# Four norms of a first model: sums and inverse of the deviation kept one token to a partition, and spread again by TensorE

## The reference, cut to what matters

```python
def rms_norm(x, g):
    xf = x.astype(jnp.float32)
    y = xf * lax.rsqrt(jnp.mean(xf * xf, axis=-1, keepdims=True) + EPS)
    return (y * g.astype(jnp.float32)).astype(x.dtype)
...
        u = modulate(rms_norm(h, g_norm1[l]), mod[:, :, 0], mod[:, :, 1])
        uc = modulate(rms_norm(hc, g_norm1[l]), modc[0], modc[1])
        pl = jnp.split(u @ w_in[l], IN_SPLITS, axis=-1)
...
        u2 = modulate(rms_norm(h, g_norm2[l]), mod[:, :, 3], mod[:, :, 4])
        h = h + mod[:, :, 5] * conv_ffn(u2, w_up[l], conv_w[l], conv_b[l], w_down[l])
        if ctx_out:
```

## Time and profile before

| | |
|---|---|
| median of 3 runs | 3943.73 us (3940.05 to 3945.64) |
| the profiled execution's own time | 3943.65 us |
| its span, first to last instruction | 3941.6 us |
| mean granted clock of TensorE | 0.992 of full |
| busy share | PE 96%, PEld 77%, DVE 57%, ACT 40%, POOL 8% |

### The profile page before, as it was taken

One profiled execution on the slowest core, in us unless ns is written; L12 is line 12 of the kernel. 1 busy time (PEld: TensorE's weight loads), 2 busy tenths in 40 slices (PEclk: granted clock), 3 DMA queues, 4 the chain that ended last, 5 costly groups with the idle time before them and its releaser, 6 DMA issues. The chain is left out here.

```text
span 3941.6 us, 53696 instructions
## 1 busy us (share of the span) xinstructions
PE 3798.9 (96%) x20466; PEld 3041.6 (77%) x20466; DVE 2258.9 (57%) x3952; ACT 1567.2 (40%) x2679; POOL 315.0 (8%) x282
## 2 busy tenths in 40 slices
PE   7999989999999999999999999999899999999998
PEld 5876568888888888875788788877578887667887
DVE  5356677874543543365733555376657626766752
ACT  3245672213431322255722344353544425354431
POOL 0100001111000001100000100114010010400001
PEclk9999999999999999999999999999999999989999
DMA  5210015571121121200022233222023222212332
GB/s 193 81 43 26 1 49 165 171 237 57 65 69 60 62 70 57 70 25 26 10 98 82 84 97 100 102 89 93 19 87 99 96 91 94 80 33 90 97 101 81
DMA packets 81208, 320.13 MB, mean 81 GB/s; under 512 B 9728, under 2 KB 9856, under 8 KB 80128
## 3 DMA queue, kind: packets, MB, share of 16 engines
q1 hardware_dynamic: 68064, 270.49, 20.7%
q0 software_dynamic: 12960, 47.19, 3.6%
HBM read 311.09 MB, written 2.10 MB: 79 GB/s over the span
## 5 line engine op out<-in xcount | busy, mean ns | idle before, releaser
L539 DVE TENSOR_TENSOR split_low<-weight_ring,split_high 128x1024 fp32r<-128x1024 f32 (+1 forms) x352 | 470.1, 1335 | 417.9 <-ACT split_high L531 417.5
L531 ACT ACTIVATE split_high<-weight_ring 128x1024 fp32r<-128x1024 f32 (+1 forms) x364 | 405.5, 1115 | 751.2 <-PE banks L1522 341.1
L1722 PE MATMUL banks<-normed_high,split_high 128*128 128x512 f32 x1040 | 405.9, 390 | 3.0 <-DVE normed_low L1665 2.2
L1722 PE MATMUL banks<-normed_high,split_low 128*128 128x512 f32 x1040 | 404.9, 389 | 0.0
L1722 PE MATMUL banks<-normed_low,split_high 128*128 128x512 f32 x1040 | 404.9, 389 | 0.0
L2020 PE MATMUL banks<-normed_high,split_high 128*128 128x512 f32 (+1 forms) x704 | 237.9, 338 | 2.8 <-DVE normed_low L1935 2.7
L2020 PE MATMUL banks<-normed_low,split_high 128*128 128x512 f32 (+1 forms) x704 | 237.2, 337 | 0.0
L2020 PE MATMUL banks<-normed_high,split_low 128*128 128x512 f32 (+1 forms) x704 | 236.7, 336 | 0.0
L1722 PEld LDWEIGHTS banks<-normed_high,split_high 128*128 128x128 f32 x1040 | 195.2, 188 | 47.4 <-DVE normed_low L1665 3.0
L1722 PEld LDWEIGHTS banks<-normed_high,split_low 128*128 128x128 f32 x1040 | 195.2, 188 | 40.6
L1722 PEld LDWEIGHTS banks<-normed_low,split_high 128*128 128x128 f32 x1040 | 195.3, 188 | 39.9
(11 more groups left out here) (388 smaller groups left out, 8599.3 us busy)
## 6 DMA issues: line engine op xcount, KB each, us to landing
weight_ring<-in_up SPq DMA_DIRECT2D x174, 512.0 KB, 3.4
weight_ring<-in_down SPq DMA_DIRECT2D x64, 704.0 KB, 4.0
modulation_ring<-in_ada POOLq DMA_DIRECT2D x80, 512.0 KB, 3.8
weight_ring<-in_merge SPq DMA_DIRECT2D x48, 768.0 KB, 4.2
weight_ring<-in_inputs SPq DMA_DIRECT2D x36, 512.0 KB, 3.4
weight_ring<-in_out SPq DMA_DIRECT2D x32, 512.0 KB, 3.4
weight_ring<-in_xbc SPq DMA_DIRECT2D x16, 512.0 KB, 3.4
weight_ring<-in_short SPq DMA_DIRECT2D x12, 512.0 KB, 3.4
```

Of the source, the lines that this page charges most:

```text
L531: act.activation(k.splits[0][:, (n0 + panel) % RING, 0:width], k.slot(n0 + panel)[:, 0:width], ACT.Copy).then_inc(k.high_ready.sem, 1)
L539: dve.tensor_tensor(k.splits[1][:, s, 0:width], k.ring[:, s, 0:width], k.splits[0][:, s, 0:width].bitcast(F32), ALU.subtract).then_inc(k.l ...
L1722: last = pe.matmul(sums(r, half), w, x, start=(c + j == 0), stop=(c == KT - 1 and j == 2))
```

## The change

Squares are now stationary, 128 tokens at a time, and one column of ones is moved: token t of a group of 128 gets its sum on partition t, in one column of PSUM (`sum_columns`, 6 matmuls per tile for 768 tokens, 4 for 512). The root and the reciprocal are taken of 6 (or 4) columns in a new buffer `deviations`. Then TensorE spreads each column to all partitions again: the column, broadcast to 128x128, is stationary, and the identity is moved, 128 columns (`spread_inverse`, a new semaphore `inverse_spread`). VectorE's scaling reads the inverse from PSUM instead of SBUF, and waits for the spread. In norm 1 each tile's sums are followed by one filler matmul. The 12, 15, 18 and 16 fillers ahead of the first products become 2+4, 3+5, 3+6 and 3+5, with the spread between. `stream_norm` (norm 4) no longer calls `norm`, which itself stays as it was. The diff, cut (the second copies of like edits and the counts of semaphores at block ends are left out):

```diff
+def norm_by_columns(k, group, ranges, split=None, modulation=None, ahead=0, block=None):
...
+    @block.scalar
+    def _(act):
+        root_of_columns(k, act, SQUARES_BANK, (b - a) // P)
+        split_ahead(k, act, ahead)
+        for q, (src, dst, gain, shift) in enumerate(group if split else ()):
...
+        if modulation:
+            modulated_gains(k, dve, *modulation)
+        invert_columns(k, dve, (b - a) // P)
+        dve.wait_ge(*k.inverse_spread(1))
+        if modulation:
+            dve.wait_ge(*k.gains_ready(1))
+        for q, (src, dst, gain, _) in enumerate(group):
+            dve.scalar_tensor_tensor(dst[:, a:b], src[:, a:b], gain(which), k.psum[:, SQUARES_BANK, 0:b - a],
+                                     ALU.mult, ALU.mult).then_inc(k.scaled_ready.sem, 1)
+            if ahead == 2 and q == 0:
+                dve.wait_ge(*k.low_ready(1))
+                split_low(k, dve, k.next_panel, 1, KT * P, k.high_ready(2))
+            if split and q:
+                low_part(q - 1)
+        if split:
...
+def sum_columns(k, pe, bank, squared, count, start, stop):
+    for t in range(count):
+        last = pe.matmul(k.psum[:, bank, t:t + 1], squared[:, t * P:(t + 1) * P], k.table("ones")[:, 0:1],
+                         start=start and t == 0, stop=stop and t == count - 1)
+    return last
+def root_of_columns(k, act, bank, count, epsilon=12, at=0):
+    act.activation(k.deviations[:, at:at + count], k.psum[:, bank, 0:count], ACT.Sqrt,
+                   bias=k.scalars[:, epsilon:epsilon + 1], scale=1.0 / D).then_inc(k.deviation_ready.sem, 1)
+def invert_columns(k, dve, count, roots=1):
+    dve.wait_ge(*k.deviation_ready(roots))
+    dve.reciprocal(k.deviations[:, 0:count], k.deviations[:, 0:count]).then_inc(k.inverse_ready.sem, 1)
+def spread_inverse(k, pe, ready, targets):
+    pe.wait_ge(*ready)
+    for bank, first, count in targets:
+        for t in range(count):
+            last = pe.matmul(k.psum[:, bank, t * P:(t + 1) * P],
+                             k.deviations[:, first + t:first + t + 1].to_broadcast([P, P]), k.table("ident"),
+                             start=True, stop=True)
+        last.then_inc(k.inverse_spread.sem, 1)
...
             for n in range(squared):
                 pe.wait_ge(*k.squares_ready(n + 1))
-                for s, (a, b) in enumerate(columns):
-                    last = pe.matmul(k.psum[:, s, 0:b - a], k.table("ones"), k.probs[:, n % 2, a:b], start=(n == 0),
-                                     stop=(n == KT - 1))
-                last.then_inc(k.squares_summed.sem, 1)
+                sum_columns(k, pe, 0, k.probs[:, n % 2, :], T // P, n == 0, n == KT - 1).then_inc(k.squares_summed.sem, 1)
+                keep_busy(k, pe, 1)
             if ada:
                 modulate()
-            keep_busy(k, pe, 12 if ada else 18)
+            keep_busy(k, pe, 2 if ada else 3)
+            spread_inverse(k, pe, k.inverse_ready(1), ((0, CTX // P, LAT // P), (1, 0, CTX // P)))
+            keep_busy(k, pe, 4 if ada else 6)
             for c in range(KT):
...
-            for s, (a, b) in enumerate(columns):
-                act.activation(k.probs[:, 2, a:b], k.psum[:, s, 0:b - a], ACT.Sqrt, bias=k.scalars[:, 12:13],
-                               scale=1.0 / D).then_inc(k.deviation_ready.sem, 1)
+            root_of_columns(k, act, 0, T // P)
...
                     dve.scalar_tensor_tensor(scaled(c)[:, a:b], k.stream[:, c, a:b], k.gains[:, 0, c, s:s + 1],
-                                             k.probs[:, 3, a:b], ALU.mult, ALU.mult).then_inc(k.scaled_ready.sem, 1)
+                                             k.psum[:, s, 0:b - a], ALU.mult, ALU.mult).then_inc(k.scaled_ready.sem, 1)
...
-                invert()
+                invert_columns(k, dve, T // P)
...
-            dve.wait_ge(*k.inverse_ready(2))
+                invert_columns(k, dve, T // P)
...
+            if by_columns:
+                sum_columns(k, pe, plain_bank, squared_tiles[:, 2, :], n // P, True, False)
+            for region, (a, b) in enumerate(() if by_columns else squared_columns):
                 pe.matmul(k.psum[:, plain_bank + region, 0:b - a], k.table("ones"), squared_tiles[:, 2, a:b], start=True,
                           stop=False)
...
-        keep_busy(k, pe, 16 if late is None else 6)
+        if late is None:
+            keep_busy(k, pe, 3)
+            spread_inverse(k, pe, k.inverse_ready(0), ((SQUARES_BANK, 0, n // P),))
+            keep_busy(k, pe, 5)
+        else:
+            keep_busy(k, pe, 6)
...
         modulated_gains(k, dve, l, 1)
+        invert_columns(k, dve, T // P)
+        dve.wait_ge(*k.gains_ready(1))
         for q, (c, s, a, b) in enumerate(units):
             if c == 0:
-                dve.wait_ge(*k.deviation_ready(s + 1))
-                if s:
-                    low_part(q - 1)
-                dve.reciprocal(k.probs[:, 3, a:b], k.probs[:, 2, a:b]).then_inc(k.inverse_ready.sem, 1)
-                dve.wait_ge(*k.inverse_ready(s + 1))
-                dve.wait_ge(*k.gains_ready(1))
+                dve.wait_ge(*k.inverse_spread(s + 1))
             dve.scalar_tensor_tensor(target[:, c, a:b], k.stream[:, c, a:b], k.gains[:, 1, c, s:s + 1],
-                                     k.probs[:, 3, a:b], ALU.mult, ALU.mult).then_inc(k.scaled_ready.sem, 1)
+                                     k.psum[:, SQUARES_BANK + s, 0:b - a], ALU.mult, ALU.mult).then_inc(
+                                         k.scaled_ready.sem, 1)
             if q == 0:
                 dve.wait_ge(*k.low_ready(1))
                 split_low(k, dve, k.next_panel, 1, KT * P, k.high_ready(2))
-            if c:
+            if q:
                 low_part(q - 1)
         low_part(len(units) - 1)
-    k.ends(deviation_ready=2, inverse_ready=2, scaled_ready=len(units), high_ready=len(units),
-           normed_ready=len(units), gains_ready=1)
+    k.ends(scaled_ready=len(units), high_ready=len(units), normed_ready=len(units), gains_ready=1)
...
-        keep_busy(k, pe, 15)
+        keep_busy(k, pe, 3)
+        spread_inverse(k, pe, k.inverse_ready(1), ((SQUARES_BANK, CTX // P, LAT // P), (SQUARES_BANK + 1, 0, CTX // P)))
+        keep_busy(k, pe, 5)
...
-            for s, (a, b) in enumerate(streams):
-                pe.matmul(k.psum[:, s, 0:b - a], k.table("ones"), k.probs[:, m, a:b], start=start, stop=not start)
+            sum_columns(k, pe, 0, k.probs[:, m, :], T // P, start, not start)
```

69 lines of the change are left out of this document (46 added, 23 removed).

## The result

The changed kernel takes 3955.47 us (median of 7 runs, 3953.26 to 3957.87), the kernel before 3943.50 (7 runs, 3939.81 to 3946.14): a ratio of 1.0034, with a 95% interval of 1.0024 to 1.0043. So by the medians the change costs 10 to 12 us. The forecast was 3959 with a range of 3944 to 3970.

The account below looks back on a forecast made before the run. TensorE was taken to bound the kernel between norms, VectorE to end last ahead of the norms' first products. Terms +17.5, -1.7, 0 and 0 gave +15.8 on 3943.65: 3959, range 3944 to 3970 (the forecast's own 3955 to 3963).

Parts of the forecast that it names:

- Norm 1: Norm 1: column sums leave the clock low, TensorE becomes last, first scaling at 67.9 instead of 50.44; +17.5.
- The row that the prediction took it from: Attention, 3479 to 3485: TensorE busy 5.84 of 6 us, 3.06 of weight loads, clock at 0.50; read as loads not lifting it.
- the blend with 0.33: Norm 1: a sum's pair at half clock priced 0.225, between ends 0.116 and a cold load's 0.33; doubling gives 0.232.
- Norm 2: Norm 2: latents 0.6 later because the clock falls, context 2.3 earlier; together -1.7.
- the latents' 1.25: Norm 2, latents: gain of 1.25 from earlier scaling, against 1.9 lost to a falling clock.
- The context's 2.3: Norm 2, context: the second reciprocal's 1.75, 0.20 ahead of it and an estimated 0.35 of waits saved, whatever the clock does.
- Norm 3: Norm 3: -2.5 from earlier scaling, cancelled by 2.5 taken for a clock fall; 0, bounds -2.5 and +1.5.
- Norm 4: Norm 4: -1.15 from earlier scaling, limited by GpSimd's low part, a clock fall weighed in; 0, bounds -1.15 and +1.5.
- the second rival: Clock stays low in norm 1 but holds in norms 2 to 4: +10.3, 3954; chance 0.14.
- The rival that the clock rises within norm 1's sums: Norm 1: clock rises at 28.0, +4.0 there; 3940.5 if held later, 3946 if lost; chance 0.16.
- the one with pairs under 0.07: Norm 1: clock rises in the sums and a pair costs 0.06, half the price taken; 3934, chance 0.03.
- the one with 0.33 a pair: Norm 1: a pair takes a cold load's 0.33, 4.9 a tile, +27.5: 3970; the slower-still cases have chance 0.09.

Follow-up runs that it names:

- e2: The changed kernel without the one filler behind each of norm 1's tiles; 3945.21 us, ratio 1.0007.
- e3: The changed kernel with seven fillers ahead of norm 1's first sums, still one filler a tile; 3950.75 us, ratio 1.0022.
- e6: As e4, but twelve fillers ahead of norm 1's sums instead of seven; 3944.95 us, ratio 1.0007.
- e8: As e5, but norm 1's wide root is turned into columns, inverted narrow and spread, with fillers only behind the spread; 3938.07 us, ratio 0.9984.
- e7: The changed kernel run again without an edit, as its second set; 3952.83 us, ratio 1.0025.
- e5: As e1, plus fillers between the two tiles' sums: three each for norms 2 and 4, two for norm 3; 3939.17 us, ratio 0.9988.
- e9: As e8, with seven fillers ahead of norm 3's sums instead of four and three between the tiles instead of two; 3934.31 us, ratio 0.9981.
- e10: As e5, with norm 3 also as in the kernel before; 3936.77 us, ratio 0.9987.
- e4: The changed kernel with seven fillers ahead of norm 1's sums and three behind each tile instead of one; 3946.89 us, ratio 1.0017.
- e1: The changed kernel with norm 1 alone as in the kernel before; 3939.03 us, ratio 0.9993.

## Why the prediction was right, and where its terms were off

**Norm 1 (forecast +17.5, measured +15.2 at the first product).** The mechanism is shown from three sides: the clock did not rise in 20 us of pairs alone (e2), it fell under pairs with one filler (e3), and at full clock the same pairs took half as long (e6). The row that the prediction took it from the earlier trace rows was weaker evidence than it said: in that stretch at 0.50 TensorE also moved wide matmuls, four of 512 columns in 2.08 us from 3481.1, and at 3485.4 the clock rose among matmuls of the same kinds. The forecast was right, but it rested on less than e2 has since given it. The sizes: the sum's pair took 0.213 at half clock instead of 0.225, a tile 3.41 instead of 3.61, eight of them 1.6 less, of which a later start and a longer first and last tile took back 0.5; that is the error in L748's start (+14.8 for +16.0). L748 lost 1.3 instead of 2.0 (11.75 long against 10.48 in e6), because the rise came 2.6 us behind its start and not 4 (no row gave the 4; the start of the kernel before took 5.0, and e2's rise came 3.6 behind the start of L748). From the turned rows' last matmul to the first scaling it took 2.50 for 2.73. The sum's pair is 0.105 at full clock (e6) and twice that, 0.213, at half. So doubling holds, and what was off is the full-clock price of 0.116, taken from a pair with 64 columns moved; the blend with 0.33 only happened to bring 0.232 nearer to the truth. What bound norm 1 before was misread too: ahead of the scaling at 50.44 stood GpSimd's low part, which ends at 49.99, and not the reciprocals, which end at 48.62 (e8). It cost the forecast nothing, since after the change TensorE is last by far.

**Norm 2 (-1.7, measured -2.5).** The two parts were sized apart and both hold roughly. The clock fell, from 978.0 to 981.4, and the latents' 1.25 went almost exactly: -0.08 in the changed kernel, -0.34 in e7, and -1.03 in e5, where it held. I had it 0.6 slower: the fall missed the sums, which took 1.39 and 1.50. The context's 2.3 was 2.40, and is the steadiest number here: the eleven profiles with norm 2 changed lie between -2.36 and -2.41. All of it falls where the prediction had it: from the latents' first product until TensorE is through with the first panels of the context and moves 512 columns again it takes 18.50 (985.14 to 1003.64) instead of 20.89 (970.75 to 991.64). At the takeover the 1.75 reciprocal is gone, and VectorE goes from the last latent tile to the first of the context without idle:

```profile
992.26 0.75 DVE L2025 SCALAR_TENSOR_TENSOR normed_low<-normed,modulations,normed_high 128x512 fp32r<-128x512 f32 x1
992.92 0.48 DVE L2034 SCALAR_TENSOR_TENSOR normed<-residual_stream,norm_gains,banks 128x256 f32<-128x256 f32 x1
993.32 0.75 DVE L2025 SCALAR_TENSOR_TENSOR normed_low<-normed,modulations,normed_high 128x512 fp32r<-128x512 f32 x1
```

**Norm 3 (0, measured +0.3).** Right for its reason in this execution: -2.5 without the clock, and the fall from 1541.2 to 1548.0 took it all:

```profile
1540.25 4.45 PE L556 MATMUL banks<-ones_and_identity,probs 128*128 128x1 f32 x24 [1.09 <-POOL probs L2192]
1545.00 2.90 PE L587 MATMUL banks<-ones_and_identity 128*128 128x256 f32 x6 [0.30 <-PEq L2309]
1547.69 1.66 PE L578 MATMUL banks<-ones_and_identity,deviations 128*128 128x128 f32 x12
```

The sums were to take 2.8 and the three fillers 1.36. e9 puts it the other way round: with the clock held and 1.36 of fillers paid, norm 3 gives 1.5. But the 0 is one outcome of two: in e2 and e3, whose norm 3 is the changed kernel's, the fall lasted 3.4 us instead of 6.8, and norm 3 gave 1.2 and 1.3. That the loss taken, 2.5 of at most 4.3, met the gain so exactly is luck.

**Norm 4 (0, bounds -1.15 and +1.5; measured -1.08 and +0.02).** Both happened, in two executions of one kernel. VectorE again waits for GpSimd's low part (0.46 idle at 2232.81), as written, and the gain is the 1.15 forecast when the clock holds. In e5, e8, e9 and e10, with fillers between the sums, it was -1.07 or -1.08 in all four. That the fillers did it is shown by e8 alone: the other three had the fall at some 1720 behind which norm 4 kept the clock in the changed kernel and e3 without any filler.

**The sum (15.8, measured 11.7 between the spans).** Norm 1 was sized 2.3 too dear, norm 2 0.8, norm 4 1.1 in this execution, norm 3 0.3 too cheap, and the stretches between give the last 0.2. So 3955.5 for 3959 comes of four errors of which three point the same way; norm 4's is chance. The second set's 3952.83 lies below the forecast's own 3955 to 3963, though in its whole range. The result near 3954 is not the second rival come true, in which the clock holds in norms 2 to 4: by the time alone the two could not be told apart, but the trace shows the falls in norms 2 and 3. The rival that the clock rises within norm 1's sums is refuted by e2 and e3; the one with pairs under 0.07 by e6's 0.105; the one with 0.33 a pair by 0.213.

**The rule that activity releases the clock**, which the prediction takes from the Trainium skill, "TensorE: Matmul & The Clock Gate", section "What's actually happening", agrees with the first rises, 2.6 and 3.6 us into L748 (changed kernel, e2). What the prediction found open in it, e2 answers for its own case: 20.5 us of back-to-back weight loads with one-column matmuls went by at half clock.

**Open.** Norm 1's first product to norm 2 and what follows norm 4 differ by up to 5 us, once 8.5, from the kernel before, in code that no edit touched. Behind norm 4 the record of the clock bears out that falls account for most of it: over the twelve profiles the stretch grows by some 0.45 us for each us spent at 0.50, from 1710.5 with 47 us (e8) to 1719.3 with 67 us (e2). Between norms 1 and 2 the seven profiles with 6.8 us at 0.50 took 904.5 to 908.1, the five with 3.4 us 902.3 to 905.3, so there the clock explains a part. Whether this is why medians differ by 1 to 2 us more than the segments say is not shown, since only one execution of each kernel was profiled. Of e4 only one of the three long executions was profiled, so that the nine others kept the clock is inferred from their times.

## What to carry to other kernels

Swapping the operands of a sum, so that the data is the stationary side and one column moves, saves no time on TensorE where the data is wide: 12 pairs took 1.26 at full clock and 2.56 at half, where wide sums of the same tile took 1.29, and the clock stayed down or fell while they ran in the changed kernel, e2 and e3. It paid where few tiles are summed and a wide reciprocal on the critical engine goes away: 2.40 in norm 2 whatever the clock did, and in norm 3 from a loss of 0.3 to a gain of 1.5, by how long the clock was down (a loss of 1.2 where fillers came on top of the fall, e5 and e8). Before pricing such a change, ask of each stretch which clock it will run at, and price fillers as part of it. A filler that does not change the clock is a plain cost: one a tile cost 7 us here. And before taking reciprocals for what binds, look at what the other engines end at the same moment: norm 1's scaling came behind GpSimd's low part.

## What the runs showed of the hardware that I had not expected

- One stream of instructions at two speeds: twelve pairs and three fillers a tile ran at 0.50 for 41 us in e4's profile, and at 1.00 to the end of norm 1 in e6's. It makes some 22 us between executions of one kernel, e4. What decides is open: the 1.27 us of idle ahead stands in e3's profile too, where the clock held for two tiles.
- With five fillers more, which push the first sums back by 1 us, the executions were 3942.6 to 3952.0 (e6) for 3941.7 to 3970.0 (e4); with three long ones in twelve that may still be chance.
- Short VectorE instructions of 128x16 and 128x20, two operands from SBUF, took 0.69 to 1.85 us instead of 0.14 to 0.18 while GpSimd's 2.35 us low part ran beside them, and ended 0.03 to 0.04 us behind it, in six profiles of six.
- A scaling whose third operand lies in PSUM took as long as one from SBUF: four in 2.19 (L907) against four in 2.21 (L915 in e1).
- In norm 3, with two fillers between the sums, four ahead and 1.09 of idle, the clock fell (e5, e8); with three and seven, which leave no idle ahead of the sums, it held in the profiled execution (e9).
